# Hybrid conv and forgetting-attention layer: x loaded by quarters, summed on rows, split factor by factor

## The chip, the core and the metric

The kernel runs on one core of a Trainium2 chip. The metric is the device time of one execution, in microseconds. The core has TensorE (PE in the profile, its weight loads PEld), VectorE (DVE), ScalarE (ACT), GpSimd (POOL) and SyncE (SP), which issues most DMAs. Each takes its own queue in order and waits for others on semaphores.

## The reference

One decoder layer on 512 tokens of width 2048, cut to what matters here:

```python
def reference(x, w_in, b_in, w_dw, b_dw, g_conv_norm, b_conv_norm, w_out, b_out, g_post, b_post):
    z = jnp.einsum("bsd,de->bse", x, w_in) + b_in        # (1, 512, 2048) x (2048, 14352)
    glu_val, glu_gate, gate_c, q, k, v, f_logit, gate_a = _split_columns(z)   # 7 x 2048 and 16 columns
    y_conv = _conformer_conv(glu_val, glu_gate, w_dw, b_dw, g_conv_norm, b_conv_norm)  # 31 taps, norm, silu
    y_conv = y_conv * jax.nn.silu(gate_c)
    y_attn = _forgetting_attention(q, k, v, f_logit)     # 16 heads, causal, logits + cum[q] - cum[k],
    y_attn = y_attn * jax.nn.silu(gate_a)                #   cum = cumsum(log_sigmoid(f_logit))
    y = jnp.concatenate([y_conv, y_attn], axis=-1)
    sub = jnp.einsum("bse,ed->bsd", y, w_out) + b_out
    return _layer_norm(DN_ALPHA * x + sub, g_post, b_post)
```

## The kernel before

**Products.** Matrix products in fp32 are made of three products of rounded halves: each operand is split into a high half (rounded by ACT) and a low half (what is left, by DVE). `mm3` (L860) issues L862 to L864. `z = x w_in` goes by groups g of two column tiles of 128 (`kinds_of`, L91; 56 groups, PAIRS: q and k of a head, then v and gate_a, then val and glu; at last gate_c). A group is one 2x2 Strassen step in Winograd's form: x is cut in quarters (tokens 0 to 255 and 256 to 511, k in 0 to 1023 and 1024 to 2047), w_in's two tiles likewise in blocks B11, B12, B22, B21, and seven products m ("units", 8 k-tiles, 24 matmuls of 128x256) replace eight. ORDER (L41) gives their order, FACTOR which of x's seven factors (a11, a12, a22, ns1, s2, s3, s4) each takes, SOURCE which block. Units are numbered through: 0 to 5 in group 0, 6 is group 1's first (m = 1), 14 is group 2's m = 2 (from B21), 15 is group 1's m = 4, computed in group 2 because its source comes last. Per slot s of a group ACT rounds the weights of the unit two ahead (`high`, L582, waits until that unit's buffer is free) and DVE makes its low half (`low`, L1087).

**Sources.** sum_1 and sum_2 (DVE, L1093, L1104) and sum_3 and sum_4 (adding DMAs from POOL's queue, L506, L513) form the block sums in a ring of seven raw tiles. Group g's unit m = 4 waits for sum_4(g) (`t4_in`). In the groups with g % 3 == 1 POOL runs `masks` (L520) between sum_3 and sum_4: it waits for the bias rows of that head and adds the causal mask.

**The head of the kernel.** x is loaded whole, in five cuts of columns (`load_x`, L376, X_CUTS). For each k (0 to 7) TensorE turns eight 128x128 tiles (`turn_x`, L904), ACT copies two banks (`x_copy`, L609), DVE forms four sums (`x_sums`, L1116), ACT rounds all seven factors at once (`x_high`, L620, 128x1792) and DVE subtracts (`x_low`, L1132). TensorE takes the ten f products of that k (F_TERMS, L936 and L938) and, from k = 3 on, unit 0's products behind each. Units 1 to 5 follow behind the last k.

**Forget values.** The 16 f columns give logits in bank R5. `forget` (ACT L645, DVE L1154) makes log-sigmoid and its running sum: steps 0 and 1 (ACT) and 0 and 3 (DVE) of group 0. Then SP (L405 to L408) stores it and loads it back over the partitions as bias rows of head 0 (`load_bias`), in front of group 2's loads. `masks(0)` waits for those four loads (`bias_loaded`), DVE's row maxima of head 0 (L1249, group 2) for the masks.

The order is written out by hand in every engine's loop over g and s; a group's loads (`loads`, L325) are issued in the order B11, B12, B22, B21, each behind the use that frees its buffer.

## Time and profile before

| | us |
|---|---|
| median of 3 runs | 1664.21 (1662.56 to 1666.98) |
| profiled execution, its own time | 1665.44 |
| its span | 1663.6 |
| TensorE busy | 1603.0 (96% of the span) |
| DVE, ACT, POOL busy | 1394.4, 795.7, 234.4 |

Durations and starts are of the profiled execution, counted from the start of its span; its own time is 1.2 us above the median. A busy TensorE is not one at its peak: its matmuls overlap, so pitch (start to start) counts, not duration. The granted clock has two levels, 2.4 GHz (1.00) and 1.2 GHz (0.50); its mean over the span is 0.986.

### The profile page before, as it was taken

How to read it: one execution, taken by the hardware profiler on the slowest of the kernel's cores; microseconds unless marked ns; L12 is line 12 of the kernel's file. 1: busy time of each engine (PE TensorE's matmuls, PEld its weight loads, DVE VectorE, ACT ScalarE, POOL GpSimd, SP SyncE). 2: the span in 40 equal slices, each digit the busy share in tenths (PEclk: the TensorE clock that was granted, in tenths of full speed). 3: DMA queues.
4: the chain of work that ended last, by engine and by line, in shares of the span. 5: the costliest groups of instructions: out<-in, count | busy, mean ns of one | idle time of the engine just before them, and what ended most of it. 6: DMA issues, size and time to landing. Idle time of an engine off the chain costs nothing. (4 is left out here: it accounts for less than half of the span.)

```text
span 1663.6 us, 29190 instructions
## 1 busy us (share of the span) xinstructions
PE 1603.0 (96%) x11718; PEld 1529.3 (92%) x11718; DVE 1394.4 (84%) x1872; ACT 795.7 (48%) x1175; POOL 234.4 (14%) x231
## 2 busy tenths in 40 slices
PE   5999999999999999999999999999978899999997
PEld 4899999999999999999999999998978788888885
DVE  6669999999999999999999999999766575663358
ACT  5555454554554545545545545454544454232240
POOL 0101101101111011011111110111222002610000
PEclk9999999999999999999999999999989999999998
DMA  5666867767677676676676676766788954434232
GB/s 159 171 143 163 177 139 166 174 146 175 157 172 171 142 178 161 138 180 159 162 181 146 169 174 141 169 145 162 208 221 216 331 174 146 164 102 152 92 111 101
DMA packets 295558, 271.88 MB, mean 163 GB/s; under 512 B 11697, under 2 KB 252497, under 8 KB 294497
## 3 DMA queue, kind: packets, MB, share of 16 engines
q1 hardware_dynamic: 278288, 203.95, 42.9%
q0 software_dynamic: 17136, 66.07, 20.6%
q8 instruction: 93, 1.52, 0.4%
q14 instruction: 41, 0.34, 0.1%
HBM read 190.26 MB, written 21.00 MB: 127 GB/s over the span
## 5 line engine op out<-in xcount | busy, mean ns | idle before, releaser
L862 PE MATMUL ps<-xh,whl 128*128 128x256 f32 x3136 | 898.1, 286 | 29.1 <-ACT nu L684 16.7
L863 PE MATMUL ps<-xl,whl 128*128 128x256 f32 x3136 | 890.7, 284 | 0.0
L864 PE MATMUL ps<-xh,whl 128*128 128x256 f32 x3136 | 890.6, 284 | 0.0
L607 ACT ACTIVATE whl<-raw 128x1024 fp32r<-128x1024 f32 x392 | 415.3, 1061 | 590.5 <-PE ps L864 459.6
L1091 DVE TENSOR_TENSOR whl<-raw,whl 128x1024 fp32r<-128x1024 f32 x448 | 564.7, 1261 | 101.2 <-ACT whl L607 83.5
L862 PEld LDWEIGHTS ps<-xh,whl 128*128 128x128 f32 x3136 | 603.2, 192 | 33.2 <-ACT nu L684 17.5
L863 PEld LDWEIGHTS ps<-xl,whl 128*128 128x128 f32 x3136 | 603.4, 192 | 0.2 <-issue 0.2
L864 PEld LDWEIGHTS ps<-xh,whl 128*128 128x128 f32 x3136 | 602.9, 192 | 0.0
L1186 DVE SCALAR_TENSOR_TENSOR c_tiles<-ps,taps,c_tiles 128x511 f32<-128x511 f32 (+14 forms) x480 | 350.5, 730 | 6.9
L862 PE MATMUL ps<-whl,yh 128*128 128x512 f32 x464 | 180.6, 389 | 0.3 <-DVE yl L1363 0.3
L864 PE MATMUL ps<-whl,yl 128*128 128x512 f32 x464 | 180.5, 389 | 0.0
L863 PE MATMUL ps<-whl,yh 128*128 128x512 f32 x464 | 180.5, 389 | 0.0
L517 POOL DMA_DIRECT2D raw<-raw x56 | 48.5, 867 | 536.5 <-DVE whl L1091 466.6
L510 POOL DMA_DIRECT2D raw<-raw x56 | 48.8, 871 | 424.0 <-DVE raw L1101 414.4
L862 PEld LDWEIGHTS ps<-whl,yh 128*128 128x128 f32 x464 | 87.1, 188 | 18.5 <-issue 0.7
L864 PEld LDWEIGHTS ps<-whl,yl 128*128 128x128 f32 x464 | 87.1, 188 | 18.2
L863 PEld LDWEIGHTS ps<-whl,yh 128*128 128x128 f32 x464 | 87.1, 188 | 18.1
L1363 DVE TENSOR_TENSOR yl<-yc,yh 128x512 fp32r<-128x512 f32 x24 | 26.3, 1094 | 57.6 <-ACT yh L806 57.6
L1101 DVE TENSOR_TENSOR raw<-raw 128x1024 f32<-128x1024 f32 x56 | 71.9, 1283 | 0.6 <-DMA raw<-in_w_in_dram 0.6
L1363 DVE TENSOR_TENSOR yl<-ya,yh 128x512 fp32r<-128x512 f32 x32 | 22.1, 691 | 59.1 <-ACT yh L806 59.1
L1109 DVE TENSOR_TENSOR raw<-raw 128x1024 f32<-128x1024 f32 x56 | 68.7, 1227 | 1.9
L806 ACT ACTIVATE yh<-ya 128x512 fp32r<-128x512 f32 x32 | 20.2, 632 | 91.0 <-PE ps L864 86.3
(191 smaller groups left out, 1357.1 us busy)
## 6 DMA issues: line engine op xcount, KB each, us to landing
raw<-in_w_in_dram SPq DMA_DIRECT2D x224, 512.0 KB, 5.4
raw<-raw POOLq DMA_DIRECT2D x112, 512.0 KB, 4.9
raw<-in_w_out_dram SPq DMA_DIRECT2D x64, 512.0 KB, 3.6
probs<-forget_sums_dram SPq DMA_DIRECT2D x16, 256.0 KB, 7.2
attn_rows_dram<-tiles SPq DMA_DIRECT2D x16, 256.0 KB, 3.7
conv_rows_dram<-c_tiles SPq DMA_DIRECT2D x16, 256.0 KB, 7.2
gate_rows_dram<-tiles SPq DMA_DIRECT2D x16, 256.0 KB, 4.9
cin<-conv_rows_dram SPq DMA_DIRECT2D x16, 256.0 KB, 3.3
```

Of the source, the lines that this page charges most:

```text
L510: nc.gpsimd.dma_start(raw[:, ring(g, B12), :], raw[:, ring(g, B22), :], accum_op=ALU.add) \
L517: nc.gpsimd.dma_start(raw[:, ring(g, SUM), :], raw[:, ring(g, B21), :], accum_op=ALU.add) \
L607: nc.scalar.activation(w_high(n), source(n), ACT.Copy).then_inc(high_done, 1)
L806: nc.scalar.activation(yh[:, t % 2, :], y_tile(k), ACT.Copy).then_inc(yh_done, 1)
L862: nc.tensor.matmul(o, ah, bh, start=start, stop=False, skip_group_check=True)
L863: nc.tensor.matmul(o, ah, bl, start=False, stop=False, skip_group_check=True)
L864: return nc.tensor.matmul(o, al, bh, start=False, stop=True, skip_group_check=True)
L1091: vec.tensor_tensor(w_low(n), src, w_high(n), ALU.subtract).then_inc(low_done, 1)
L1101: vec.tensor_tensor(raw[:, ring(g, SUM), :], raw[:, ring(g, B11), :], raw[:, ring(g, B12), :], ALU.add).then_inc(t1_done, 1)
L1109: vec.tensor_tensor(o, o, raw[:, ring(g, B22), :], ALU.add).then_inc(t2_done, 1)
L1186: vec.scalar_tensor_tensor(out=o[:, n:], in0=ps[:, U_BANK, 0:SEQ - n], scalar=tap, in1=o[:, n:], op0=ALU.mult, op1=ALU.add) \
L1363: vec.tensor_tensor(yl[:, t % 2, :], y_tile(t % PER_PASS), yh[:, t % 2, :], ALU.subtract).then_inc(yl_done, 1)
```

## The change

1. x is loaded by quarters of two token tiles by 1024 columns (x11, x12, x21, x22), with the weight blocks in between; SP no longer waits for the turned and split x before dw_rows and group 1's loads.
2. The sums are formed on rows, before turning: x22 - x21 (ns1) and s2 by DVE in `x_sums`, s3 and the negative of s4 by POOL, each one operation of 128x2048. Turned are then all seven factors, in 28 banks of two k-tiles.
3. A factor's bank goes from PSUM straight to its high half (ACT, 128x512) and low half (DVE, 128x512). X_ORDER sets the order; the turns of the next factor stand between the products of units 0, 2, 3, 4 and 5, those of ns1 behind unit 1. Group 1's first unit waits for all 28.
4. f's products are regrouped so that they need factors 0, 1, 3 and 5 (with the sum of the two halves of w_f as a third weight and its negative as a fourth), each behind a unit of group 0; they end behind unit 4, in bank U_BANK. `forget` moves to group 1: ACT at s = 0 and 2, DVE at s = 1 and 3. SP's store and bias loads of head 0 move between B22 and B21 of group 2.
5. Row tiles, f_w and dw_rows lie elsewhere in memory; taps turn into R2 instead of BANK_A.

The core of the diff (declarations left out):

```diff
...
-X_CUTS = ((0, 1), (1, 2), (2, 4), (4, 6), (6, 8))
+X_ORDER = (0, 1, 3, 4, 6, 5, 2)
+X_BANKS = 4 * len(X_ORDER)
...
                     sp.wait_ge(low_done, at(g - 1, 1) + 1)
                     sp.wait_ge(t1_done, g)
                 load_block(g, B22, 1, 1)
+                if g == 2:
+                    sp.wait_ge(f_vec, 4)
+                    sp.dma_start(scratch, neg_cum[0:HEADS, :]).then_inc(cum_stored, 16)
+                    sp.wait_ge(cum_stored, 16)
+                    load_bias(0)
...
+            def load_x(q, dst, tokens, half):
+                for h in range(2):
+                    c = slice(SEQ * h, SEQ * (h + 1))
+                    src = x[0, tokens:tokens + TOK, 1024 * half + SEQ * h:1024 * half + SEQ * (h + 1)]
+                    sp.dma_start(dst[:, :, c], src.rearrange("(t p) d -> p t d", p=P)).then_inc(x_loaded[q][h], 16)
+            load_x("11", x11, 0, 0)
+            load_block(0, B11, 0, 0)
...
-            load_x(1)
+            load_x("12", x12, 0, 1)
...
+            load_block(0, B21, 1, 0)
+            load_x("21", x21, TOK, 0)
             load_block(0, B12, 0, 1)
+            load_x("22", x22, TOK, 1)
             load_block(0, B22, 1, 1)
-            load_block(0, B21, 1, 0)
             sp.dma_start(fbias[:, :], b_in[F_COL:F_COL + HEADS].rearrange("(j p) -> j p", p=1)).then_inc(fbias_loaded, 16)
-            sp.wait_ge(xt_turned, HALF)
             sp.dma_start(dw_rows[0:TAPS, :], w_dw).then_inc(dw_loaded, 16)
-            sp.wait_ge(xl_done, HALF)
             loads(1)
-            sp.wait_ge(f_vec, 4)
-            sp.dma_start(scratch, neg_cum[0:HEADS, :]).then_inc(cum_stored, 16)
-            sp.wait_ge(cum_stored, 16)
-            load_bias(0)
             for g in range(2, GROUPS):
                 loads(g)
...
+            pool.wait_ge(x_loaded["21"][0], 16)
+            pool.wait_ge(x_loaded["21"][1], 16)
+            pool.wait_ge(xt_turned, 4)
+            nc.gpsimd.tensor_tensor(x11[:, :, :], x11[:, :, :], x21[:, :, :], ALU.subtract).then_inc(s3_done, 1)
...
             for g in range(GROUPS):
                 sum_3(g)
+                if g == 0:
+                    pool.wait_ge(s2_done, 1)
+                    nc.gpsimd.tensor_tensor(x12[:, :, :], x12[:, :, :], x21[:, :, :], ALU.add).then_inc(s4_done, 1)
...
-            def x_copy(k):
-                act.wait_ge(xt_turned, k + 1)
-                if k >= 2:
-                    act.wait_ge(xl_done, k - 1)
...
-            def x_high(k):
-                act.wait_ge(x_summed, 4 * k + 4)
-                nc.scalar.activation(xh[:, :, k, :], x_tmp[k % 2][:, 1:8, :], ACT.Copy).then_inc(xh_done, 1)
-            for k in range(HALF + 1):
-                if k < HALF:
-                    x_copy(k)
-                if k >= 1:
-                    x_high(k - 1)
...
+            def x_high(f):
+                at_f = 4 * X_ORDER.index(f)
+                for b in range(4):
+                    act.wait_ge(xt_turned, X_BANKS if f == 2 else at_f + b + 1)
+                    nc.scalar.activation(xh[:, f, 2 * b:2 * b + 2, :].rearrange("p k t -> p (k t)"), ps[:, x_bank(at_f + b), :],
+                                         ACT.Copy, scale=-1.0 if f == 6 else 1.0).then_inc(xh_done, 1)
+            x_high(0)
+            high(0)
+            act.wait_ge(f_loaded, 32)
+            nc.scalar.activation(f_w[:, 0:2, :, 0:HEADS].rearrange("p a k c -> p (a k) c"),
+                                 f_raw[:, :, :, :].rearrange("p a k c -> p (a k) c"), ACT.Copy).then_inc(fw_high, 1)
+            act.wait_ge(f_summed, 1)
+            nc.scalar.activation(f_w[:, 2, :, 0:HEADS], f_sum[:, :, :], ACT.Copy).then_inc(fw_high, 1)
+            act.wait_ge(fw_low, 2)
+            act.wait_ge(vec_const, 3)
+            nc.scalar.activation(f_w[:, 3, :, :], f_w[:, 2, :, :], ACT.Copy, scale=-1.0).then_inc(fw_done, 1)
+            x_high(1)
             high(1)
...
@@ -773,15 +779,23 @@
                     n = slot_unit(g, s)
                     if n is not None:
                         high(n + 2)
-                    if g == 0 and s in (0, 1):
+                    if g == 0 and s == 0:
+                        x_high(3)
+                        x_high(4)
+                    if g == 1 and s in (0, 2):
                         forget(s)
                     evict(g, s)
+                    if g == 0 and s == 1:
+                        x_high(6)
+                    if g == 0 and s == 4:
+                        x_high(5)
                     attention(g, s)
...
+                    if g == 0 and s == 6:
                         act.wait_ge(taps_turned, 1)
...
+                if g == 1 and m == 1:
+                    pe.wait_ge(xl_done, X_BANKS)
                 for k in range(HALF):
+                    if g == 0 and m != 4 and k % 2 == 0:
+                        pe.wait_ge(xl_done, 4 * X_ORDER.index(FACTOR[m]) + k // 2 + 1)
                     last = product(n, k)
+                    if g == 0 and m in (1, 5, 6, 3, 7) and k % 2:
+                        turn_x(X_ORDER[X_ORDER.index(FACTOR[m]) + 1], k // 2)
...
+            def turn_x(f, b):
+                j = 4 * X_ORDER.index(f) + b
+                if f in quarter and b % 2 == 0:
+                    pe.wait_ge(x_loaded[quarter[f]][b // 2], 16)
+                if f in made and b == 0:
+                    pe.wait_ge(made[f], 1)
+                if j >= 4:
+                    pe.wait_ge(xl_done, j - 3)
+                for kk in range(2):
+                    for tile in range(2):
+                        o, k = TOK * kk + P * tile, 2 * b + kk
+                        last = nc.tensor.transpose(ps[:, x_bank(j), o:o + P], x_rows_of[f][:, tile, P * k:P * (k + 1)],
+                                                   ident[:, :])
                 last.then_inc(xt_turned, 1)
...
+            def f_terms(terms, first=False):
+                for w, f, r in terms:
+                    c = slice(TOK * r, TOK * (r + 1))
+                    pe.wait_ge(xl_done, 4 * X_ORDER.index(f) + 4)
+                    for k in range(HALF):
+                        nc.tensor.matmul(ps[0:F_WIDE, U_BANK, c], f_w[:, w, k, :], xh[:, f, k, :],
+                                         start=first and (w, k) == (0, 0), stop=False, skip_group_check=True)
+                        last = nc.tensor.matmul(ps[0:HEADS, U_BANK, c], f_w[:, w, k, 0:HEADS], xl[:, f, k, :],
...
+                return last
...
+            for b in range(4):
+                turn_x(0, b)
+            unit(0)
...
+            pe.wait_ge(fw_done, 1)
+            f_terms(((0, 0, 0), (2, 0, 1)), True)
...
                     if g == 0 and s == 1:
+                        for b in range(4):
+                            turn_x(3, b)
+                        f_terms(((1, 1, 0),))
+                    if g == 0 and s == 3:
+                        f_terms(((1, 3, 1),))
+                    if g == 0 and s == 5:
                         pe.wait_ge(dw_loaded, 16)
+                        pe.wait_ge(c11_done, 1)
                         for c in range(HEADS):
...
                         last.then_inc(taps_turned, 1)
+                        f_terms(((3, 5, 1),)).then_inc(f_done, 1)
...
-            def x_sums(k):
-                t = x_tmp[k % 2]
-                a21, a11, a12, a22, ns1, s2, s3, s4 = (t[:, n, :] for n in range(8))
...
-            def x_low(k):
-                dve.wait_ge(xh_done, k + 1)
-                vec.tensor_tensor(xl[:, :, k, :], x_tmp[k % 2][:, 1:8, :], xh[:, :, k, :], ALU.subtract).then_inc(xl_done, 1)
...
+            def x_low(f):
+                at_f = 4 * X_ORDER.index(f)
+                if f == 2:
+                    dve.wait_ge(taps_turned, 1)
+                for b in range(4):
+                    dve.wait_ge(xh_done, at_f + b + 1)
+                    hi = xh[:, f, 2 * b:2 * b + 2, :].rearrange("p k t -> p (k t)")
+                    lo = xl[:, f, 2 * b:2 * b + 2, :].rearrange("p k t -> p (k t)")
+                    if f == 6:
+                        vec.scalar_tensor_tensor(out=lo, in0=ps[:, x_bank(at_f + b), :], scalar=-1.0, in1=hi,
+                                                 op0=ALU.mult, op1=ALU.subtract).then_inc(xl_done, 1)
+                    else:
+                        vec.tensor_tensor(lo, ps[:, x_bank(at_f + b), :], hi, ALU.subtract).then_inc(xl_done, 1)
...
+            x_low(0)
+            low(0)
+            dve.wait_ge(f_loaded, 32)
+            vec.tensor_tensor(f_sum[:, :, :], f_raw[:, 0, :, :], f_raw[:, 1, :, :], ALU.add).then_inc(f_summed, 1)
+            dve.wait_ge(fw_high, 2)
...
+            x_low(1)
+            low(1)
             sum_1(0)
...
+            def x_sums():
+                for h in range(2):
+                    dve.wait_ge(x_loaded["21"][h], 16)
+                    dve.wait_ge(x_loaded["22"][h], 16)
+                vec.tensor_tensor(xs1[:, :, :], x22[:, :, :], x21[:, :, :], ALU.subtract).then_inc(ns1_done, 1)
+                dve.wait_ge(ns1_done, 1)
+                dve.wait_ge(s3_done, 1)
+                vec.scalar_tensor_tensor(out=x21[:, :, :], in0=x11[:, :, :], scalar=-1.0, in1=x22[:, :, :],
+                                         op0=ALU.mult, op1=ALU.subtract).then_inc(s2_done, 1)
...
@@ -1340,13 +1367,24 @@
                     conv(i, before)
                     if n is not None:
                         low(n + 2)
+                        if n == 0:
+                            x_sums()
+                            x_low(3)
                         if n + 2 < UNITS and UNIT_OF[n + 2][1] == 5:
                             sum_2(UNIT_OF[n + 2][0])
+                        if n == 0:
+                            x_low(4)
+                        if n == 1:
+                            x_low(6)
                     if s == 5 and g < GROUPS - 1:
                         sum_1(g + 1)
-                    if g == 0 and s in (0, 3):
+                    if g == 1 and s in (1, 3):
                         forget(s)
                     evict(g, s)
+                    if g == 0 and s == 4:
+                        x_low(5)
+                    if g == 0 and s == 6:
+                        x_low(2)
...
```

**SP, from group 1's B11 on.** `raw<-in_w_in_dram` are w_in's blocks, `forget_sums_dram` the running sums. Before:

```order
L321 DMA raw<-in_w_in_dram 128x8x128
L321 DMA raw<-in_w_in_dram 128x8x128 [waits t1_done,low_done]
L321 DMA raw<-in_w_in_dram 128x8x128 [waits t3_in0,low_done]
L406 DMA forget_sums_dram<-neg_cum 16x512 [waits f_vec]
L352 DMA probs<-forget_sums_dram 128x128 [waits cum_stored]
L352 DMA probs<-forget_sums_dram 128x256
L352 DMA probs<-forget_sums_dram 128x384
L352 DMA probs<-forget_sums_dram 128x512
L321 DMA raw<-in_w_in_dram 128x8x128 [waits low_done]
L321 DMA raw<-in_w_in_dram 128x8x128 [waits t4_in0]
```

In the changed kernel (from group 2's B11; group 1's four stand ahead of it):

```order
L332 DMA raw<-in_w_in_dram 128x8x128 [waits t3_in0,low_done]
L332 DMA raw<-in_w_in_dram 128x8x128 [waits low_done]
L332 DMA raw<-in_w_in_dram 128x8x128 [waits t4_in0]
L332 DMA raw<-in_w_in_dram 128x8x128 [waits t1_done,low_done]
L350 DMA forget_sums_dram<-neg_cum 16x512 [waits f_vec]
L368 DMA probs<-forget_sums_dram 128x128 [waits cum_stored]
L368 DMA probs<-forget_sums_dram 128x256
L368 DMA probs<-forget_sums_dram 128x384
L368 DMA probs<-forget_sums_dram 128x512
L332 DMA raw<-in_w_in_dram 128x8x128 [waits t3_in1,low_done]
L332 DMA raw<-in_w_in_dram 128x8x128 [waits low_done]
```

Behind group 1's loads stood the store and the bias loads; now B11, B12 and B22 of group 2 go first, and B21 waits behind them.

**POOL's queue at the start.** L510 (now L518) is sum_3, L517 (now L525) sum_4, `probs<-probs,mask` the masks of head 0. Before:

```order
L510 DMA raw<-raw 128x1024 [waits b22_in0,t1_done,const_done]
L517 DMA raw<-raw 128x1024 [waits b21_in0,low_done]
L510 DMA raw<-raw 128x1024 [waits b22_in1,t1_done]
L525 TENSOR_TENSOR probs<-probs,mask 128x128 [waits bias_loaded]
L525 TENSOR_TENSOR probs<-probs,mask 128x128 x3
L517 DMA raw<-raw 128x1024 [waits b21_in1,low_done]
L510 DMA raw<-raw 128x1024 [waits b22_in0,t1_done]
```

In the changed kernel:

```order
L555 TENSOR_TENSOR x<-x 128x2048 [waits x21_loaded1,xt_turned,x21_loaded0,const_done]
L518 DMA raw<-raw 128x1024 [waits b22_in0,t1_done]
L561 TENSOR_TENSOR x<-x 128x2048 [waits s2_done]
L525 DMA raw<-raw 128x1024 [waits b21_in0,low_done]
L518 DMA raw<-raw 128x1024 [waits b22_in1,t1_done]
L533 TENSOR_TENSOR probs<-probs,mask 128x128 [waits bias_loaded]
L533 TENSOR_TENSOR probs<-probs,mask 128x128 x3
L525 DMA raw<-raw 128x1024 [waits b21_in1,low_done]
```

Two sums of x came in, one ahead of sum_3(0) and one behind it; masks(0) and sum_4(1) stand as they did.

**DVE around the forget values.** L1091 (now L1117) is `low`, L1109 (now L1133) sum_2. Before, in group 0, from sum_2(0) on:

```order
L1109 TENSOR_TENSOR raw<-raw 128x1024 [waits b22_in0,low_done]
L1159 SCALAR_TENSOR_TENSOR f_tmp<-ps,fbias,f_low 16x512 [waits fbias_loaded,f_act]
L1091 TENSOR_TENSOR whl<-raw,whl 128x1024 [waits high_done] x2
L1163 SCALAR_TENSOR_TENSOR c_tiles<-f_tmp 16x512 [waits f_act]
L1167 SCALAR_TENSOR_TENSOR c_tiles<-csum,c_tiles 16x512 [waits f_vec,vec_const]
L1169 TENSOR_SCALAR neg_cum<-c_tiles 16x512 [waits f_vec]
L1170 MEMSET csum 128x512
L1211 TENSOR_TENSOR tiles<-ps,p 128x256 [waits unit_done,p1_done]
```

In the changed kernel, in group 1, behind its sum_2 (L1263 is k's low half, L1238 the eviction c11):

```order
L1186 SCALAR_TENSOR_TENSOR f_tmp<-ps,fbias,f_low 16x512 [waits fbias_loaded,f_act]
L1117 TENSOR_TENSOR whl<-raw,whl 128x1024 [waits high_done]
L1263 TENSOR_TENSOR parts<-tiles,parts 128x512 [waits kh_done]
L1117 TENSOR_TENSOR whl<-raw,whl 128x1024 [waits high_done]
L1190 SCALAR_TENSOR_TENSOR c_tiles<-f_tmp 16x512 [waits f_act]
L1194 SCALAR_TENSOR_TENSOR c_tiles<-csum,c_tiles 16x512 [waits f_vec,vec_const]
L1196 TENSOR_SCALAR neg_cum<-c_tiles 16x512 [waits f_vec]
L1197 MEMSET csum 128x512
L1238 TENSOR_TENSOR tiles<-ps,p 128x256 [waits unit_done,p1_done]
L1117 TENSOR_TENSOR whl<-raw,whl 128x1024 [waits high_done] x2
```

The three operations on 16 partitions moved from behind low(4) to behind low(11).

## Rows read from the trace of the kernel before

**Rows 1.** What TensorE waited for up to 68 us: total, times, longest

```profile
PE ps L936 <- DVE xl L1134: 10.8, 6, 2.6
PE ps L913 <- DMA x_rows<-in_x_dram: 9.1, 3, 4.7
```

**Rows 2.** Windows: busy per engine (x instructions), PEclk, DMA share, GB/s

```profile
2.00:25.00 23.00, 12.90 (x65) 10.55 (x66) 13.01 (x22) 11.21 (x19) 0.00 (x0) 1.00 1.01 281
4.63:67.20 62.57, 45.66 (x306) 40.35 (x307) 44.73 (x59) 35.80 (x46) 2.46 (x3) 0.92 0.56 152
...
95.03:1120.00 1024.97, 1024.97 (x8448) 1020.95 (x8447) 981.53 (x1382) 536.90 (x833) 144.23 (x169) 1.00 0.69 161
```

**Rows 3.** Timeline of TensorE: start, us, engine, line, op, tiles [idle before]

```profile
4.66 1.09 PE L913 MATMUL ps<-ident,x_rows 128*128 128x128 f32 x4 [4.66 <-DMA x_rows<-in_x_dram]
...
24.66 0.32 PE L936 MATMUL ps<-xh,f_w 128*48 128x256 f32 x1 [2.60 <-DVE xl L1134]
...
25.87 0.60 PE L913 MATMUL ps<-ident,x_rows 128*128 128x128 f32 x4
26.30 0.60 PE L916 MATMUL ps<-ident,x_rows 128*128 128x128 f32 x4
...
67.20 0.28 PE L862 MATMUL ps<-xh,whl 128*128 128x256 f32 x1
...
89.27 0.28 PE L862 MATMUL ps<-xh,whl 128*128 128x256 f32 x1
...
95.03 0.29 PE L862 MATMUL ps<-xh,whl 128*128 128x256 f32 x1
```

**Rows 4.** Groups by shape, ACT and DVE: count, busy us, mean ns

```profile
L607 ACT ACTIVATE whl<-raw 128x1024 fp32r<-128x1024 f32 x392 | 415.3, 1061 | 590.5 <-PE ps L864 459.6 <-DVE raw L1109 73.7 <-DMA raw<-in_w_in_dram 46.9
L720 ACT ACTIVATE vh<-ps 128x512 fp32r<-128x512 f32 x16 | 9.3, 582 | 0.0
...
L1109 DVE TENSOR_TENSOR raw<-raw 128x1024 f32<-128x1024 f32 x56 | 68.7, 1227 | 1.9
L1265 DVE TENSOR_TENSOR vl<-ps,vh 128x512 fp32r<-128x512 f32 x16 | 11.0, 685 | 0.0
L1134 DVE TENSOR_TENSOR xl<-w_even,xh 128x1792 fp32r<-128x1792 f32 x4 | 8.1, 2026 | 0.0
```

**Rows 5.** Timeline of POOL and DVE where both run on SBUF

```profile
1441.10 4.60 POOL L573 TENSOR_TENSOR res<-res,bout_b 128x2048 f32<-128x2048 f32 x1
...
1441.26 5.53 DVE L1091 TENSOR_TENSOR whl<-raw,whl 128x1024 fp32r<-128x1024 f32 x1 [0.26 <-ACT whl L588]
```

**Rows 6.** Windows around 1210 us, columns as in Rows 2

```profile
1204.40:1210.00 5.60, 0.00 (x1) 0.01 (x1) 0.52 (x2) 1.48 (x3) 0.00 (x0) 0.75 1.01 265
1210.00:1214.00 4.00, 4.00 (x18) 4.00 (x19) 3.66 (x3) 0.46 (x1) 1.44 (x1) 0.50 1.09 285
```

**Rows 7.** Timeline of the forget chain: ACT, DVE, SP and POOL

```profile
53.80 0.62 ACT L652 ACTIVATE f_tmp<-f_tmp 16x512 f32<-16x512 f32 x1
...
56.39 0.72 ACT L656 ACTIVATE f_tmp<-f_tmp,one 16x512 f32<-16x512 f32 x1
...
59.73 0.67 DVE L1163 SCALAR_TENSOR_TENSOR c_tiles<-f_tmp 16x512 f32<-16x512 f32 x1
...
62.20 0.33 SPq L406 DMA_DIRECT2D forget_sums_dram<-neg_cum  x1
63.80 1.77 SPq L352 DMA_DIRECT2D probs<-forget_sums_dram  x4
...
72.37 2.85 POOL L525 TENSOR_TENSOR probs<-probs,mask 128x128 f32<-128x128 f32 x4 [4.83 <-DMA probs<-forget_sums_dram]
76.71 0.87 POOL L517 DMA_DIRECT2D raw<-raw  x1 [1.49 <-DVE whl L1091]
```

**Rows 8.** L517, POOL's sum_4, by source line

```profile
DMA to landing us min/median/max: 4.5/4.9/7.4
```

**Rows 9.** The page's DMA issues: count, KB each, us to landing

```profile
raw<-in_w_in_dram SPq DMA_DIRECT2D x224, 512.0 KB, 5.4
```

170 lines of the change are left out of this document (49 added, 121 removed).

## The prediction

> **What bounds the kernel now.** I read the waits of TensorE first. Up to 68 us it waits 10.8 us for DVE's low halves of x and 9.1 us for x itself [rows 1]. The windows come next. While the loads run (2 to 25 us) the DMA engines move 281 GB/s; between 4.63 and 67.20 TensorE is busy for 45.66 of 62.57 us; from 95.03 to 1120 it is busy all the time, and DVE for 981.53 of 1024.97 us [rows 2]. So what is gained or lost before 95 us moves the end by as much: a dense TensorE can't catch up. Last, TensorE's timeline [rows 3]: the first transposes start at 4.66, group 1's first unit (unit 6 from 0; I call its start U) at 67.20, unit 13 behind the first head's scores at 89.27, unit 15 at 95.03. A unit takes (95.03 - 89.27)/2 = 2.88 us at the higher of the clock's two levels, and unit 15 starts at U + 27.83. Any change has to be judged by two numbers: where U goes, and whether unit 15 still starts at U + 27.8.
>
> **The head, part by part.** What goes: eight steps, one for each k, in which a bank pair is turned, copied (ACT), summed (DVE), rounded (ACT) and subtracted (DVE, 2.03 us [rows 4]); TensorE only does f products and two turns in a step (24.66 to 26.9, then it waits [rows 3]). What comes: 28 banks (7 factors, 4 banks each), 112 transposes instead of 64, in banks of 0.43 us (26.30 - 25.87 [rows 3]), so 12.0 us; the 80 f products stay, at 0.12 us each (ten between 24.66 and 25.87 [rows 3]); six units, 17.3 us. A bank costs ACT 0.58 us and DVE 0.68 us [rows 4], of which some 0.1 overlaps the next. The sums on rows are two DVE operations of 128x2048, 2.3 us each by the 1792 elements in 2.03 us [rows 4], and two on POOL, 4.6 us each [rows 5].
>
> Landings: x's first 0.52 MB before are there at 4.66; after that I count bytes at 281 GB/s [rows 2, 3]. In the new order: x11 6.5, block B11 8.4, x12 12.6, B21 14.8, x21 18.5, B12 20.3, x22 24.1, B22 25.9.
>
> The queues, followed in this order, give:
> - Unit 0 starts when B11's low half is made: ACT ends xh of factor 0 near 9.1, rounds B11 to 10.1 and DVE subtracts to 11.3 (1.06 and 1.23 us [rows 4]). TensorE is at the lower clock there. I let it rise near 16.5. Unit 0 with four banks ends at 18.3, the f products of factor 0 at 22.5.
> - POOL's first sum runs from 18.5 (x21) to 23.1. DVE's low half of B21 wants to start at 20.1. What two such operations do to each other stands in [rows 5]: a DVE operation on two SBUF inputs, started 0.16 us behind a POOL sum of 4.60 us, took 5.53 us instead of 1.2. So it ends at 24.3: unit 1 runs 24.4 to 27.3.
> - sum_1 25.5, high and low of unit 2 to 27.8, x22 - x21 to 30.1, the next sum to 32.4. TensorE waits 2.8 us for factor 3. DVE: low halves of factor 3 to 34.9; then sum_2, which POOL's second sum (32.4 to 37.0) holds to 38.2; factor 4 to 40.7; low(3) to 41.9. Unit 2 and its banks end at 38.3, f at 40.2, wait 1.8.
> - Unit 3 with factor 6's banks 42.0 to 46.6. ACT takes high(4) only behind all four banks, so low(4) ends at 49.7 and the eviction before unit 4 at 49.9: wait 3.3. Unit 4 to 54.5, taps and f to 57.8, unit 5 to 62.4. Unit 6 waits for all 28 banks: four of ACT and four of DVE behind the last turn, to 65.7: wait 3.3.
>
> So U = 65.7 with the clock high from 16.5 on. In a gap of 5.60 us the clock fell, and the 4 us behind it, at the lower level (0.50), held 18 matmuls, where 0.12 us each makes 33 [rows 6]: nearly 2 us lost. Four gaps of 1.8 to 3.3 us follow here; I add 2.5 us, with 0 and 8 as ends. **U = 68.2, against 67.2: +1.0.** Lowest: no hold by POOL (-3.2 and -1.2 us) and no fall of the clock, U near 61; highest 74.
>
> On the hold the Trainium skill (SBUF — State Buffer, section "SBUF: two separate sides") says that the shared port pair is an exclusive lock, taken by a DVE operation only with two SBUF inputs or in a 2-port mode. By that the low halves read from PSUM go free, as I have them; no row here shows that pair. Were they held as well, factor 3's would end at 39.5 instead of 34.9, and U would be some 4 us later: inside my upper end.
>
> **The forget chain.** It is the part of the change that looks free. It moves from group 0 (steps 0 and 3) into group 1 (ACT at 0 and 2, DVE at 1 and 3), and its end, the four bias loads, moves behind B22 of group 2. Before, the last forget operation ended and the store was issued at 62.20, U - 5.0; the masks began on POOL at 72.37, U + 5.2, and sum_4(1) was issued at 76.71, U + 9.5 [rows 7]. POOL's queue is unchanged: masks(0), then sum_4(1), the source of unit 15 (its t4_in). Now, from U on:
> - high(9) waits for unit 6: U + 3.1 to 4.2; low(9) 5.5, sum_2(1) 6.6, the bias sum of f 7.3.
> - ACT's Abs, Exp, table load and Ln take 57.11 - 53.80 = 3.3 us [rows 7], behind high(10) at 7.7: to U + 11.0. high(11) to 12.1, low(11) to 13.3.
> - DVE's three forget operations end where the store is issued, 62.20 - 59.73 = 2.47 us [rows 7]: U + 15.75. Low(12) stands behind them and ends at 17.9; unit 12 loses 0.6 us.
> - Store to masks 10.2 us, masks 2.85 [rows 7]: U + 28.8. Issue to landing of such a sum 4.9 us [rows 8]: U + 33.7. High, low and c22, which unit 15 waits for too, 2.75 us (1.06, 1.23 and some 0.4 for c22 and the hand-overs): U + 36.45.
>
> Unit 15 was due at U + 27.8, so **8.6 us**. Part of it shows one unit earlier: B21 of group 2 stands in SP's queue behind the bias loads, so it is issued no sooner than 65.57 - 62.20 = 3.4 us behind the forget end [rows 7], at U + 19.1; with the 5.4 us of such a load [rows 9] and the bias loads ahead of it I take U + 27.5, where unit 14, due at U + 25.5, needs it 2.3 us earlier: it waits some 4 us. Behind unit 15 ACT and DVE have lost their lead of two units: the row maxima, Exp and high(17) follow one another there; I add 1.1 us (0 to 2.5), my estimate of what stands between. The two gaps, 4 and 3 us, cost clock as in [rows 6]: 1.5 (0 to 3.5). **Together +11.2.** Ends: landing 4.5 to 7.4 [rows 8], masks without contention 1 us less, bias loads 2 us quicker on an emptier queue, no clock loss: +6; the other way +16.
>
> Nothing hides it: DVE's position behind low(11) alone (unit 9's start + 2.6 + 2.45 = U + 13.7) leaves 5 us of stall with every other term at its lower end. B21 of group 2 lost its cover for the same reason.
>
> **The rest** costs nothing: POOL had 1.5 us idle before sum_4 and has no other early work; dw_rows, fbias and the cols come long before use; memory is only laid out anew.
>
> **Sum.** The profiled execution took 1665.4 us (span 1663.6), 1.2 above the median. 1665.4 + 1.0 + 11.2 = 1677.6; less 1.2, **1676 us**, about 0.7% slower.
>
> **Rivals.**
> - Both terms at their low side (0.17): U near 62 to 64, stall +7: the head's gain pays for the stall, 1660 to 1668. For it: 16.9 us of waits in the head really exist. Against: seven factors one behind the other, each with an ACT and a DVE pass before the next unit.
> - The head gets dense (0.08). If TensorE never waited behind the start of unit 0, the rest of the head would take only its own work: 10.3 us of turns, 9.6 of f, 2 small, 17.3 of units and 3 of low clock, 42 us from 11.3: U = 53. Then -14 + 10 = -4, 1660, and with the stall at 5, 1655. It decides for faster from U below about 56. Against it: the waits found above are bare chains, ACT behind a bank and DVE behind ACT, with no other work that could give way.
> - Worse than forecast (0.13): the PSUM readers are held too and every gap costs clock, 1683 to 1692. Here also belongs a sentence of the Trainium skill (TensorE: Matmul & The Clock Gate, "Part 4: PE-mode transpose"), by which transposes don't lift the clock. Row 24.66 to 26.30 speaks against it (f products and turns alone, at 0.12 us a matmul); were it so, the head's 40 us of work would double and the result pass 1690.
> - The change doesn't do what it says (0.02): the forget values are wanted later than I think, no stall; then only U's shift counts, 1665.
>
> **How the numbers follow.** Forecast 0.60. The range 1662 to 1684 leaves out the dense head and the worst case, about 0.2. A measurement of this kernel can tell 0.3% from no change, 5 us. Faster by more: 0.08. Within: 0.20 (the first and last rival, and the forecast's edge). Slower: 0.72.
>
> **What would show it.** The store of the forget sums some 16 us behind unit 6's start, masks near U + 26, and TensorE idle before units 14 and 15 by 7 to 9 us together, released by a low half behind DMA. In the head: unit 6 between 65 and 70, DVE operations of 3 to 6 us beside POOL's two sums, waits before units 3, 4 and 6. I am wrong if unit 15 starts by U + 30, or if U is below 60.

## The result

The changed kernel took 1676.97 us (median; 1673.43 to 1678.42), the kernel before, on the same chip, 1665.17 (1662.56 to 1668.28). The ratio is 1.0067, with a 95% interval of 1.0049 to 1.0086: 11 us slower, 8 to 14. The prediction said 1676, slower. The profiled execution has a span of 1674.8 us, against 1663.6. All medians here are of executions in the chip's fast state; one slow execution of the kernel called "masks last" below (2605.86 us) is left out.

What TensorE waited for up to 115 us in the changed kernel (total, times, longest), where the kernel before had 10.8 us for low halves of x, 9.1 us for x (both [rows 1]) and 1.6 us for low halves of weights. In all it is 25.4 us for 21.5, only 3.9 more, so waiting alone doesn't make up 11 us. The five longest:

```profile
PE ps L876 <- DVE whl L1117: 9.9, 4, 4.7
PE ps L938 <- DMA x<-in_x_dram: 4.8, 1, 4.8
PE ps L876 <- DVE xl L1153: 3.4, 1, 3.4
PE ps L876 <- ACT p L683: 2.9, 1, 2.9
PE ps L938 <- DVE xs L1175: 2.7, 1, 2.7
```

L938 is a turn, L876 the first matmul of a product; `xl` is a low half of x, `whl` a low half of weights, `xs` the row sum ns1, `p` an eviction by ACT. The first row holds four waits, the longest of 4.7 us. It stands in group 2. TensorE's timeline, its starts in the head and in group 2, against [rows 3]:

```profile
24.57 0.38 PE L876 MATMUL ps<-xh,whl 128*128 128x256 f32 x1 [1.86 <-DVE whl L1117]
...
30.39 3.57 PE L938 MATMUL ps<-ident,xs 128*128 128x128 f32 x16 [2.69 <-DVE xs L1175]
...
43.35 0.36 PE L876 MATMUL ps<-xh,whl 128*128 128x256 f32 x1 [1.06 <-ACT p L671]
...
51.13 0.58 PE L876 MATMUL ps<-xh,whl 128*128 128x256 f32 x1 [2.94 <-ACT p L683]
...
68.82 0.55 PE L876 MATMUL ps<-xh,whl 128*128 128x256 f32 x1 [3.37 <-DVE xl L1153]
...
101.51 0.36 PE L876 MATMUL ps<-xh,whl 128*128 128x256 f32 x1 [4.70 <-DVE whl L1117]
...
106.39 0.38 PE L876 MATMUL ps<-xh,whl 128*128 128x256 f32 x1 [0.28 <-DVE tiles L1254]
```

These are unit 1, the turns of factor 3, units 3, 4 and 6, then 14 and 15. Unit 6, U of the prediction, starts at 68.82 (before 67.20, +1.62). Unit 15 starts at 106.39, U + 37.57, where it was U + 27.83: so 9.74 us are lost between the two: 4.70 in one wait before unit 14, only 0.28 before unit 15 (for c22, behind low(15)), and the other 4.8 because TensorE ran slower. Of these, 3.0 stand between U and that wait (unit 6 alone took 5.25 us for 2.88), 1.7 in unit 14. The windows, against [rows 2]:

```profile
2.00:25.00 23.00, 15.43 (x93) 14.21 (x94) 12.40 (x15) 8.18 (x17) 4.60 (x1) 1.00 1.03 300
66.00:70.00 4.00, 1.18 (x5) 1.22 (x6) 3.81 (x6) 3.08 (x6) 0.00 (x0) 0.73 0.01 3
68.82:74.00 5.18, 5.18 (x24) 5.18 (x25) 1.31 (x2) 0.28 (x1) 0.00 (x0) 0.50 0.62 167
70.00:90.00 20.00, 19.99 (x150) 19.81 (x149) 11.63 (x15) 10.82 (x15) 0.00 (x0) 0.88 0.32 83
100.00:105.00 5.00, 3.49 (x18) 3.52 (x19) 1.77 (x3) 1.41 (x3) 0.83 (x1) 0.70 0.97 184
115.00:1130.00 1015.00, 1014.94 (x8363) 1010.68 (x8362) 974.49 (x1373) 529.00 (x817) 144.29 (x167) 1.00 0.69 162
```

Columns as in rows 2. The loads ran at 300 GB/s instead of 281. The clock column is the new thing: 0.73 around unit 6's wait, 0.50 over unit 6 itself (the row of 5.18 us), 0.88 over 70 to 90 us, 0.70 around unit 14's wait. From 115 us on TensorE is dense again.

A landmark for the middle of the kernel is POOL's sum_4 of group 20 (the rows of before, then of after):

```profile
493.58 0.86 POOL L517 DMA_DIRECT2D raw<-raw  x1 [11.66 <-DMA raw<-in_w_in_dram]
```

```profile
506.25 0.86 POOL L525 DMA_DIRECT2D raw<-raw  x1 [11.64 <-DVE whl L1117]
```

It stands 12.67 us later, and so do those of groups 10, 40 and 49, to 0.02 us: nothing is gained or lost in the dense part. I call this the **dense shift** and use it below, because it is free of what the last 450 us do. Behind 1176 us, where both kernels wait for loads again, 1.5 us are given back in these two executions (span +11.2). Other kernels below give back more, or lose some: a dense shift and a time can differ by some 3 us.

### The profile page after: what moved, and what is told of

It is laid out like the page before. It is cut to its first block and busy times, and to the rows that moved or that the text cites. A ratio compares the mean times of both kernels' runs of the same rounds, so it can differ in the third digit from the quotient of the medians.

```text
span 1674.8 us, 29286 instructions
## 1 busy us (share of the span) xinstructions
PE 1612.9 (96%) x11766; PEld 1540.7 (92%) x11766; DVE 1397.8 (83%) x1863; ACT 790.2 (47%) x1180; POOL 242.7 (14%) x233
## 5 line engine op out<-in xcount | busy, mean ns | idle before, releaser
L876 PE MATMUL ps<-xh,whl 128*128 128x256 f32 x3136 | 903.5, 288 | 42.4 <-ACT nu L690 13.9
L623 ACT ACTIVATE whl<-raw 128x1024 fp32r<-128x1024 f32 x392 | 415.0, 1060 | 591.8 <-PE ps L878 448.4
L1117 DVE TENSOR_TENSOR whl<-raw,whl 128x1024 fp32r<-128x1024 f32 x448 | 565.7, 1263 | 108.7 <-ACT whl L623 88.6
L876 PEld LDWEIGHTS ps<-xh,whl 128*128 128x128 f32 x3136 | 606.6, 193 | 48.1 <-ACT nu L690 14.7
L876 PE MATMUL ps<-whl,yh 128*128 128x512 f32 x464 | 180.6, 389 | 0.3 <-DVE yl L1401 0.3
L525 POOL DMA_DIRECT2D raw<-raw x56 | 48.5, 866 | 533.9 <-DVE whl L1117 475.7
L876 PEld LDWEIGHTS ps<-whl,yh 128*128 128x128 f32 x464 | 87.1, 188 | 18.7 <-issue 0.7
L518 POOL DMA_DIRECT2D raw<-raw x56 | 49.1, 876 | 379.3 <-DVE raw L1125 369.6
L1401 DVE TENSOR_TENSOR yl<-yc,yh 128x512 fp32r<-128x512 f32 x24 | 30.7, 1281 | 53.4 <-ACT yh L820 53.4
L1133 DVE TENSOR_TENSOR raw<-raw 128x1024 f32<-128x1024 f32 x56 | 70.6, 1260 | 1.9
L604 ACT ACTIVATE whl<-raw 128x1024 fp32r<-128x1024 f32 x56 | 58.5, 1046 | 13.2 <-DMA raw<-in_w_out_dram 13.2
```

The source lines that it names most:

```text
L518: nc.gpsimd.dma_start(raw[:, ring(g, B12), :], raw[:, ring(g, B22), :], accum_op=ALU.add) \
L525: nc.gpsimd.dma_start(raw[:, ring(g, SUM), :], raw[:, ring(g, B21), :], accum_op=ALU.add) \
L604: nc.scalar.activation(w_high(n), raw_out(t), ACT.Copy).then_inc(high_done, 1)
L623: nc.scalar.activation(w_high(n), source(n), ACT.Copy).then_inc(high_done, 1)
L876: nc.tensor.matmul(o, ah, bh, start=start, stop=False, skip_group_check=True)
L1117: vec.tensor_tensor(w_low(n), src, w_high(n), ALU.subtract).then_inc(low_done, 1)
```

## The forget chain in the trace

From ACT's Ln to unit 15's weights in the changed kernel: ACT's Ln, the first of DVE's last three operations, SP's store and B21 of group 2 (with the four loads behind it), POOL's masks and sum_4(1), ACT's high(14), and high(15) with high(16). It answers to [rows 7]:

```profile
81.54 0.72 ACT L662 ACTIVATE f_tmp<-f_tmp,one 16x512 f32<-16x512 f32 x1
...
84.39 0.67 DVE L1190 SCALAR_TENSOR_TENSOR c_tiles<-f_tmp 16x512 f32<-16x512 f32 x1
...
86.85 0.33 SPq L350 DMA_DIRECT2D forget_sums_dram<-neg_cum  x1
...
90.31 24.52 SPq L332 DMA_DIRECT2D raw<-in_w_in_dram  x5
...
97.47 1.68 POOL L533 TENSOR_TENSOR probs<-probs,mask 128x128 f32<-128x128 f32 x4 [34.94 <-DMA probs<-forget_sums_dram]
99.11 0.84 POOL L525 DMA_DIRECT2D raw<-raw  x1
...
99.05 1.06 ACT L623 ACTIVATE whl<-raw 128x1024 fp32r<-128x1024 f32 x1 [11.51 <-DMA raw<-in_w_in_dram]
103.69 2.00 ACT L623 ACTIVATE whl<-raw 128x1024 fp32r<-128x1024 f32 x2 [3.59 <-DMA raw<-raw]
```

Set against the prediction, from U = 68.82: store U + 18.0 (said 15.75), masks U + 28.65 (25.95), end of the masks U + 30.3 (28.75), sum_4(1) landed and high(15) started U + 34.9 (33.7), unit 15 U + 37.57 (36.45). The chain is the one that was described. The store is 2.3 us late because unit 6 ran at the lower clock (0.50 from 68.82 to 74.00), and high(9), low(9) and all behind them wait for unit 6's end. The masks took 1.68 us instead of 2.85, which gives 1.2 back.

B21 of group 2 was issued at 90.31 and high(14) could read it at 99.05, U + 30.2 (said 27.5). So unit 14 waited 4.70 us, and then ran at the lower clock (0.70 from 100 to 105); by the time that it ended sum_4(1) had landed. The wait that I had put in front of both units in equal parts stood nearly whole in front of unit 14. Which of the two chains is the longer can't be told from that trace, since each hides the other. That is what the first experiments are for.

## Experiments on the forget chain

**Only the late chain.** The kernel before, its head untouched, with the end of the forget chain moved as in the change:

```diff
@@ SP, in loads(g), behind B22; taken out behind loads(1)
+                if g == 2:
+                    sp.wait_ge(f_vec, 4)
+                    sp.dma_start(scratch, neg_cum[0:HEADS, :]).then_inc(cum_stored, 16)
+                    sp.wait_ge(cum_stored, 16)
+                    load_bias(0)
@@ ACT
-                    if g == 0 and s in (0, 1):
+                    if (g, s) in ((0, 0), (1, 2)):
                         forget(s)
@@ DVE
-                    if g == 0 and s in (0, 3):
+                    if (g, s) in ((0, 0), (1, 3)):
                         forget(s)
```

> The kernel before with only the end of the forget chain moved as the change moves it: ACT's Abs, Exp and Ln to group 1's slot 2, DVE's three operations to slot 3, store and bias loads of head 0 between B22 and B21 of group 2. x's loading and the head stay. Theory (the late forget chain stalls group 2 by itself): unit 6 stays at 67 us, the store stands at 83, masks(0) at 93, unit 14 and unit 15 wait for 7 to 9 us together; 8 to 11 us above the kernel before, 1673 to 1676. Rival (the loss comes from the new head, the forget chain has cover): within 3 us of the kernel before.

It took 1671.04 us beside 1665.49 of before (ratio 1.0040, 1.0028 to 1.0052); dense shift 7.92. Unit 6, store, masks and unit 14:

```profile
66.00 0.28 PE L863 MATMUL ps<-xh,whl 128*128 128x256 f32 x1
...
81.62 0.33 SPq L339 DMA_DIRECT2D forget_sums_dram<-neg_cum  x1
...
92.77 1.69 POOL L526 TENSOR_TENSOR probs<-probs,mask 128x128 f32<-128x128 f32 x4 [27.67 <-DMA probs<-forget_sums_dram]
...
96.61 0.55 PE L863 MATMUL ps<-xh,whl 128*128 128x256 f32 x1 [5.04 <-DVE whl L1092]
```

The late chain alone makes the kernel slower, and by the same two waits (5.04 before unit 14, 0.67 before unit 15). Together they are 5.7 us; I expected 7 to 9. The stall is 7.9 us in the dense part, or 9.1 counted from unit 6, which started 1.2 us earlier (66.00) than in the kernel before; I expected 8 to 11 over the whole time, and 5.6 were measured. Unit 6 ran at the higher clock here, and the store stood 15.62 us behind it, as the prediction has it (15.75). 3.7 us of the 7.9 are given back behind 1200 us in the profiled execution (its last sum_4 is only 4.25 later than that of before), where the kernel waits for loads and not for TensorE.

**The chain early.** The changed kernel, with the forget steps where ACT and DVE idle:

```diff
@@ ACT
-                    if g == 1 and s in (0, 2):
-                        forget(s)
+                    if g == 1 and s == 0:
+                        forget(2)
@@ ACT, g == 0 and s == 6, behind taps
+                        forget(0)
                         x_high(2)
@@ DVE
-                    if g == 1 and s in (1, 3):
-                        forget(s)
                     evict(g, s)
+                    if g == 1 and s == 0:
+                        forget(3)
@@ DVE, g == 0 and s == 6
+                        forget(1)
                         x_low(2)
```

> The changed kernel with the forget chain started as soon as its logits are there: ACT's copy and DVE's first operation ahead of factor 2's halves in group 0, the rest in slot 0 of group 1, where both engines idle for 5 us. Queues of SP and POOL as in the changed kernel. Theory: the store stands near 74, masks near 84.5, no unit waits before unit 17; of the shift of 12.7 us only the head's 1.6 and the low clock behind unit 6 (2.6) stay: 1667 to 1671. Rival (the bias loads in front of B21, or the masks in front of sum_4, cost wherever the chain ends): above 1674.

1669.74 us (ratio 1.0021, 1.0011 to 1.0031), dense shift 3.79. Store, masks and the only wait of TensorE between 69 and 120 us:

```profile
74.05 0.33 SPq L350 DMA_DIRECT2D forget_sums_dram<-neg_cum  x1
...
86.50 3.74 POOL L533 TENSOR_TENSOR probs<-probs,mask 128x128 f32<-128x128 f32 x4 [24.09 <-DMA probs<-forget_sums_dram]
...
104.22 0.35 PE L877 MATMUL ps<-xh,whl 128*128 128x256 f32 x1 [0.21 <-DVE whl L1118]
```

With the queues of SP and POOL as the change has them, 8.9 us of the 12.67 are gone. The order on those queues costs next to nothing as long as the forget values come in time. What stays, 3.8 us, is unit 6's start (68.70, +1.5), the low clock in unit 6 (4.44 us for 2.88, +1.6) and 0.7 us behind unit 15, whose cause I didn't follow up.

**B21 first; masks last; both.** On the changed kernel, with the late chain left as it is:

```diff
@@ SP (first and third kernel): the four lines of store and load_bias(0) behind, not ahead of
                 load_block(g, B21, 1, 0)
@@ POOL (second and third kernel)
-                if g < HEAD_GROUPS and g % 3 == 1:
+                if g < HEAD_GROUPS and g % 3 == 1 and g > 1:
                     masks(g // 3)
                 sum_4(g)
+                if g == 1:
+                    masks(0)
```

> The changed kernel with B21 of group 2 issued before the store and the bias loads. Theory (two chains hang on the forget values): unit 14 waits 1 us at most, unit 15 then waits some 5 for sum_4(1) and starts near 106 as before; time within 2 us of the changed kernel, 1675 to 1678. Rival (B21's place in SP's queue is the whole stall, as unit 14's wait of 4.7 us in the trace suggests): 5 to 7 us faster, 1670 to 1672.

1677.43 us (1.0071, 1.0056 to 1.0086), no faster than the change, as expected. The wait has moved to unit 15:

```profile
103.57 0.58 PE L876 MATMUL ps<-xh,whl 128*128 128x256 f32 x1 [5.56 <-DVE tiles L1254]
```

> The changed kernel with masks(0) behind sum_4(1) on POOL and nothing else. Theory (two chains side by side, of which unit 14's through B21 is as long): sum_4(1) lands before unit 15 is due, but unit 14 still waits 4 to 5 us for B21 and its low half; only the later waits shrink: dense part 0.5 to 2.5 us earlier than in the changed kernel for the same start of unit 6, time 1674 to 1677. Rival (POOL's order is the whole stall): 1668 to 1671, as with both edits.

1674.57 us (1.0057, 1.0038 to 1.0076), the median of three. The wait before unit 14 is as long as it was:

```profile
99.73 0.36 PE L878 MATMUL ps<-xh,whl 128*128 128x256 f32 x1 [4.60 <-DVE whl L1119]
```

> The changed kernel with B21 of group 2 ahead of the store and with masks(0) behind sum_4(1) on POOL. Theory: both chains to units 14 and 15 are cut; a third stays, the row maxima of head 0 on DVE wait for the masks until 99 instead of 92 and hold the low half of unit 16 and 17: a stall of 1 to 4 us, 1668 to 1673. Rival (the row maxima have no lead to lose either): as slow as the changed kernel, 1675 or more.

1669.85 us (1.0028, 1.0019 to 1.0038); the profiled execution, 1667.21, is its fastest. The only wait of TensorE in group 2:

```profile
101.85 0.35 PE L878 MATMUL ps<-xh,whl 128*128 128x256 f32 x1 [0.16 <-DVE whl L1119]
```

The head of these kernels is the same, but their unit 6 starts at different times (below), so the dense shift is read from U: (dense shift) - (U - 67.20).

| kernel | U | dense shift | from U | span |
|---|---|---|---|---|
| changed kernel | 68.82 | 12.67 | 11.05 | +11.2 |
| late chain alone | 66.00 | 7.92 | 9.12 | +4.7 |
| B21 first | 67.14 | 10.16 | 10.22 | +12.2 |
| masks last | 67.15 | 9.10 | 9.15 | +9.2 |
| both | 66.00 | 1.43 | 2.63 | +1.8 |
| chain early | 68.70 | 3.79 | 2.29 | +4.9 |

(The late chain alone has the head of the kernel before. The span is that of the profiled execution, less 1663.6.)

From U, one edit alone brings 0.8 or 1.9 us, both together 8.4. (The spans tell less: B21 first loses 2.0 us behind the dense part, where the changed kernel gains 1.5.) So there are two chains side by side behind the forget values, bias loads to B21 to unit 14 and bias loads to masks to sum_4(1) to unit 15, about 1 us apart in length (10.22 and 9.15 from U); either keeps the stall when the other is cut. The third, the row maxima that wait for the masks, has cover: with both edits no cost can be told from the early chain's (2.63 beside 2.29 from U, one execution each; I had allowed 1 to 4), though the masks ran from 93.26 to 95. I had expected them up to 99; unit 6 was early in this execution, so the edit was tried less hard than planned. Two kernels set the forget chain's own price from U: 11.05 - 2.29 = 8.8 us in the changed kernel, 9.1 alone.

## Experiments on the head

A DVE operation that is kept from running by one on POOL I call held. What DVE and POOL do beside each other in the changed kernel, against [rows 5]:

```profile
18.83 4.60 POOL L555 TENSOR_TENSOR x<-x 128x2048 f32<-128x2048 f32 x1 [16.96 <-PE ps L938]
...
20.26 4.25 DVE L1117 TENSOR_TENSOR whl<-raw,whl 128x1024 fp32r<-128x1024 f32 x1 [0.26 <-ACT whl L623]
...
32.75 4.59 POOL L561 TENSOR_TENSOR x<-x 128x2048 f32<-128x2048 f32 x1 [5.72 <-DVE x L1178]
...
32.58 2.74 DVE L1153 TENSOR_TENSOR xl<-ps,xh 128x512 fp32r<-128x512 f32 x4
35.23 3.19 DVE L1133 TENSOR_TENSOR raw<-raw 128x1024 f32<-128x1024 f32 x1
```

Low(1) started at 20.26 with POOL's s3 running until 23.43, and ended at 24.51, 1.08 behind POOL's end. Sum_2 started at 35.23, POOL's s4 ended at 37.34, sum_2 at 38.42, again 1.08 behind. In [rows 5] it is 1446.79 - 1445.70 = 1.09. Wherever it starts, the operation of 128x1024 ends the same 1.08 or 1.09 us behind POOL's end, a little less than the 1.22 it takes alone. So it doesn't run slower beside POOL, it waits and then runs. The four low halves of x between them read PSUM and took 2.74 us beside POOL's sum; in a kernel below they took 2.47 wholly beside one (34.61, without s3 in the loads' time) and in the last kernel 2.47 without one (34.24): not held. This is the pair that no row of before showed. It agrees with the Trainium skill (SBUF — State Buffer, "SBUF: two separate sides"), by which a VectorE operation takes the shared lock only with two SBUF inputs or in a 2-port mode.

**Without s3.**

```diff
-            nc.gpsimd.tensor_tensor(x11[:, :, :], x11[:, :, :], x21[:, :, :], ALU.subtract).then_inc(s3_done, 1)
+            nc.gpsimd.tensor_tensor(x11[:, 0, 0:P], x11[:, 0, 0:P], x21[:, 0, 0:P], ALU.subtract).then_inc(s3_done, 1)
```

> The changed kernel with POOL's first sum (s3) cut from 128x2048 to 128x128 elements, so part of factor 5 is left out; nothing else changed. Theory (the SBUF sum on POOL holds DVE's operation on two SBUF inputs): low(1) takes 1.2 us instead of 4.25, unit 1 starts at 22.7 instead of 24.57, factor 3's turns at 27.6 instead of 30.39, unit 6 two to three us earlier than with the same clock. Rival (the 4.25 us come from the loads' traffic): low(1) stays above 3 us and factor 3's turns start near 30.

Low(1) and the turns of factor 3:

```profile
20.98 1.23 DVE L1117 TENSOR_TENSOR whl<-raw,whl 128x1024 fp32r<-128x1024 f32 x1 [0.26 <-ACT whl L623]
...
28.08 1.97 PE L938 MATMUL ps<-ident,xs 128*128 128x128 f32 x16 [1.78 <-DVE xs L1175]
```

Low(1) takes 1.23 us, the turns start 2.3 us earlier (28.08 for 30.39), unit 6 at 65.43. That is 3.4 earlier than in the changed kernel, but 1.7 earlier than in "B21 first" and "masks last" (67.14, 67.15), whose turns of factor 3 also took 1.97 us: the hold is worth some 2 us here, the rest is clock. The traffic of the loads was the same (341 GB/s from 18 to 25 us, 340 with s3), so the hold, not the loads, made the 4.25 us. The one profiled execution took 1674.1 us.

**High(4) and low(4) early.** On the kernel with the early chain:

```diff
@@ ACT (DVE likewise, with low(4) and x_low(6)); skipped in slot 3
                     if g == 0 and s == 1:
+                        high(4)
                         x_high(6)
```

> The changed kernel with the forget chain early (as in e2_forget_early) and with high(4) and low(4) ahead of factor 6's halves on ACT and DVE, where both engines idle. Theory: the 2.9 us of wait in front of unit 4 fall to 1 or less, unit 6 starts near 66.5, time 1667 to 1669. Rival (the chain turn, high, low of factor 6 sets unit 4's start by itself): same as e2_forget_early within 1 us, 1669 to 1671.

1668.41 us (1.0018, 1.0009 to 1.0028), dense shift 2.97, beside 3.79 with the early chain alone. In time the two can't be told apart. Unit 4 still waits 2.00 us, where I expected 1 or less, and unit 6 starts at 67.88, not 66.5:

```profile
50.02 0.39 PE L879 MATMUL ps<-xh,whl 128*128 128x256 f32 x1 [2.00 <-ACT p L683]
```

It waited for low(4) no more, but for the eviction of p5, which ACT takes behind factor 6's four halves and high(5). The edit freed one of two things in the row.

**s3 out of the loads' time.** Also on the early chain:

```diff
@@ DVE, x_sums: s2 from ns1, with low(2) ahead of it
-                dve.wait_ge(s3_done, 1)
-                vec.scalar_tensor_tensor(out=x21[:, :, :], in0=x11[:, :, :], scalar=-1.0, in1=x22[:, :, :],
+                low(2)
+                vec.scalar_tensor_tensor(out=x21[:, :, :], in0=xs1[:, :, :], scalar=-1.0, in1=x11[:, :, :],
@@ POOL, behind s4; factor 5 is then turned with its sign changed, as factor 6 is
+                    nc.gpsimd.tensor_tensor(x11[:, :, :], x21[:, :, :], x22[:, :, :], ALU.add).then_inc(s3_done, 1)
```

> The changed kernel with the forget chain early and with POOL's s3 taken out of the loads' time: s2 is formed by DVE from ns1 and x11, and POOL forms the negative of s3 (s2 + x22) behind s4; low(2) stands behind ns1. Theory: low(1) is not held, factor 3's turns start near 26.5, unit 2 near 31 instead of 35.6; POOL's two sums then lie side by side at 30 to 39 and hold sum_2 and low(3), which gives 1 to 2 us back. Unit 6 at 63 to 65, time 1663 to 1666. Rival (the landing of x22 sets factor 3, not the hold): turns of factor 3 at 28 or later, time 1668 or more.

1668.78 us (1.0024, 1.0013 to 1.0036); unit 6 at 66.78, outside the 63 to 65 and the 1663 to 1666 that I expected. Half of the theory held: the turns of factor 3 started at 25.52 and unit 2 at 29.67, five to six us earlier. The gain went here:

```profile
29.02 4.58 POOL L556 TENSOR_TENSOR x<-x 128x2048 f32<-128x2048 f32 x1 [1.28 <-DVE x L1178]
33.57 5.53 POOL L558 TENSOR_TENSOR x<-x 128x2048 f32<-128x2048 f32 x1
...
31.24 3.44 DVE L1133 TENSOR_TENSOR raw<-raw 128x1024 f32<-128x1024 f32 x1
34.61 2.47 DVE L1153 TENSOR_TENSOR xl<-ps,xh 128x512 fp32r<-128x512 f32 x4
37.00 3.18 DVE L1117 TENSOR_TENSOR whl<-raw,whl 128x1024 fp32r<-128x1024 f32 x1
...
40.28 0.55 PE L876 MATMUL ps<-xh,whl 128*128 128x256 f32 x1 [3.95 <-issue]
```

Sum_2 is held to POOL's first end (33.60 + 1.08 = 34.68), low(3) to its second (39.10 + 1.08 = 40.18), and unit 3 waits 3.95 us for it. I had allowed 1 to 2. The second sum took 5.53 us instead of 4.58, and sum_2 ran in its first 1.1 us: this looks like POOL waiting for DVE in the same way. Two sums back to back cost DVE two holds, and POOL one.

**Both, and unit 6 behind one bank.** The two edits together, and

```diff
@@ PE, unit(n); factor 2's banks are turned in the order R1_ODD, BANK_A, BANK_B, BANK_C
                 if g == 1 and m == 1:
-                    pe.wait_ge(xl_done, X_BANKS)
+                    pe.wait_ge(xl_done, X_BANKS - 3)
+                if g == 0 and m == 4:
+                    pe.wait_ge(xl_done, X_BANKS)
```

> e7_no_s3_first and e9_high4 together, and unit 6 waits for the one bank of factor 2 that shares its PSUM bank, not for all four (the first product of factor 2, unit 8, waits for the rest). Theory: unit 6 at 58 to 62 and no wait in group 2, time 1656 to 1661, below the kernel before. Rival (the head stays a chain of seven factors, one ACT and one DVE pass each, whatever stands beside it): unit 6 above 64, 1663 or more.

1665.18 us (0.9996, 0.9986 to 1.0007): level with the kernel before. Units 3, 4 and 6:

```profile
40.58 0.35 PE L880 MATMUL ps<-xh,whl 128*128 128x256 f32 x1 [3.97 <-issue]
...
48.97 0.39 PE L880 MATMUL ps<-xh,whl 128*128 128x256 f32 x1 [1.99 <-ACT p L684]
...
63.49 0.36 PE L880 MATMUL ps<-xh,whl 128*128 128x256 f32 x1 [1.57 <-DVE xl L1159]
```

Unit 6's wait fell from 3.37 to 1.57, as meant; the gap before unit 3 (3.97) and the eviction before unit 4 (1.99) stayed. Unit 6 at 63.49 is outside the 58 to 62 that I expected, and the time above the 1656 to 1661. Both gaps had names by now, so one more kernel takes them away.

**No hold, p5 early.**

```diff
@@ POOL, behind sum_3(0); s4 is taken out here
+                    pool.wait_ge(low_done, 5)
+                    pool.wait_ge(x_loaded["22"][1], 16)
+                    nc.gpsimd.tensor_tensor(x11[:, :, :], s2_rows[:, :, :], x22[:, :, :], ALU.add).then_inc(s3_done, 1)
@@ DVE, behind sum_2(0); s2_rows, which s2 now goes to, lies where factor 5's low half comes later
+                            dve.wait_ge(s2_done, 1)
+                            vec.tensor_tensor(x12[:, :, :], x12[:, :, :], s2_rows[:, :, :], ALU.add).then_inc(s4_done, 1)
                             x_low(4)
@@ ACT, g == 0 and s == 1 (skipped in slot 4)
+                        evict(0, 4)
                         high(4)
                         x_high(6)
```

> e8_head with no POOL sum beside a DVE operation on two SBUF inputs: s2 goes to memory of its own (where factor 5's low half comes later), DVE forms the negative of s4 behind sum_2, POOL forms the negative of s3 behind low(4), while DVE only reads PSUM; and ACT evicts p5 right behind p1, ahead of factor 6's halves. Theory (the 4 us gap of e8_head in front of unit 3 is the hold of sum_2 and low(3), the 2 us in front of unit 4 is the eviction behind high(5)): unit 3 starts near 38.7, unit 4 without a wait of more than 0.5, unit 6 at 59 to 61, time 1659 to 1662. Rival (with the hold gone the turn, high, low chain of factors 4 and 6 is as late): unit 6 above 62.5, 1664 or more.

1658.45 us beside 1666.15 of before (ratio 0.9960, 0.9946 to 0.9975), dense shift -7.60. DVE from sum_2 on, units 3 and 6:

```profile
30.91 1.21 DVE L1141 TENSOR_TENSOR raw<-raw 128x1024 f32<-128x1024 f32 x1
32.04 2.28 DVE L1386 TENSOR_TENSOR x<-x,s_rows 128x2048 f32<-128x2048 f32 x1
34.24 2.47 DVE L1161 TENSOR_TENSOR xl<-ps,xh 128x512 fp32r<-128x512 f32 x4
...
37.95 0.36 PE L882 MATMUL ps<-xh,whl 128*128 128x256 f32 x1 [1.94 <-issue]
...
57.52 0.36 PE L882 MATMUL ps<-xh,whl 128*128 128x256 f32 x1 [1.57 <-DVE xl L1161]
```

Sum_2 takes 1.21 us, s4 on DVE 2.28; unit 3 starts at 37.95 behind 1.94 us of waiting, unit 4 without a wait, unit 6 at 57.52; both are earlier than the 38.7 and the 59 to 61 that I expected, and the time is below the 1659 to 1662. The two gaps are read apart by their rows: unit 3 came 2.6 us earlier than in e8_head (40.58), and the 1.99 us in front of unit 4 are gone. This kernel loads and sums x as the change does, and is by the medians 18.5 us faster than the changed kernel and 7.7 faster than the one before. From U it still loses 2.1 us (-7.60 for a unit 6 that is 9.68 earlier), at a clock of 1.00 from 68 to 95 us; I didn't follow that up.

## Why the prediction was right, and where its terms were off

- **Direction and size.** 1676 was forecast, 1677.0 measured; +12.2 by its sum and 12.67 in the dense part. Two terms, U and the stall, were to make it up, and they did. The stretch behind 1176 us was put at nothing and gave 1.5 us back; that the number came within 1 us has some luck in it, here and in the stall below.
- **U: +1.0 said, +1.62 measured.** The queues' ledger held to some tenths for 30 us: unit 0 at 11.3 (11.37), low(1) to 24.3 (24.5), unit 1 24.4 (24.57), factor 3's turns 30.1 (30.39). The clock rose where the text let it: unit 0's matmuls followed one another every 0.21 us up to 16.4 us, every 0.12 behind. (The clock column reads 1.00 over all of 2 to 25 us, so it doesn't show this stretch.) Units 3 and 4 came at 43.35 and 51.13 for 42.0 and 49.9, though their waits were 1.06 and 2.94 for 1.8 and 3.3. The 2.5 us set aside for clock come out as 3.1 if all that the sum leaves open (68.82 - 65.7) is put down to it.
- **The clock at U is no constant.** Kernels with this head started unit 6 at 66.00, 67.14, 67.15, 68.70 and 68.82. Two places make the difference. From factor 3's turns to unit 2 it took 5.26 us in the two late ones, whose turns came behind a wait of 2.7 us, and 3.7 in the three others, behind one of 1.2. And from unit 4 to unit 5 it took 8.2 us in the first, 9.4 to 9.7 in the others. The ends 61 to 74 held them all.
- **The stall: 8.6 said from U to unit 15, 9.74 measured.** Behind it came 1.31 (12.67 - 11.36), where the sum added 1.1 for the lost lead and 1.5 for clock. So +11.2 met 11.05 because one term was 1.1 too small and the other two together 1.3 too large; that they cancel is luck. The mis-sized step is the one from U to the store, 2.3 us too short: it counted unit 6 at the higher clock, right behind a wait for which the same text charged low clock. The late chain alone bears this out: its unit 6 ran at the higher clock, and its store came at U + 15.62 for 15.75. Shorter masks took half of the 2.3 back. The clock of the two gaps was charged on top, where it doesn't belong: unit 14 did take 106.39 - 101.51 - 0.28 = 4.6 us instead of 2.88, but sum_4(1) was still on its way, so unit 15 lost nothing more by it.
- **A share that isn't the forget chain's.** The sum gave all of the 11.2 to it. With the chain early, 2.3 us from U are still lost, 1.6 of them in unit 6's low clock. The text charged the clock of all four gaps of the head to U, but what the gap before unit 6 costs falls behind U; in the changed kernel it is also what made the store late.
- **Where the stall stands.** "It waits some 4 us" for unit 14 was 4.70. That unit 15 would wait as long again was wrong, for B21 landed 2.7 us later than the text had it. The sign "TensorE idle before units 14 and 15 by 7 to 9 us together" failed with it: 4.98 were measured, and slower running filled the rest. The two chains are nearly the same length, so the sum came near with either as the last.
- **The cover.** "Nothing hides it" is borne out by the two kernels that have the late chain with one link cut, and by the late chain alone, which costs 9.1 us from U on the old head.
- **The rivals.** The low side of both terms would need U at 62 to 64; no run with this head has it. The dense head was given 0.08, "bare chains, with no other work that could give way". For this order of work that is so, but as a statement on the head it is too strong: e10_best reaches U = 57.5 with the same loads, the same 28 banks and the same f products. The waits were chains of order (a sum beside another, an eviction behind four halves, a wait for four banks where one counts), of which I had seen the first and taken it as given. The third rival's doubled head, with transposes that don't lift the clock, did not come: from 33 to 43 us, turns, products and f products mixed, the granted clock was 0.96. No run here has turns alone for more than some 4 us, so what they do by themselves is not shown.

## What to carry to other kernels

A step moved behind "its first use is far away" must be followed to every queue that stands behind it: here a store of 16 rows held two units by two different queues, and cutting either alone brought next to nothing. Place large GpSimd operations on SBUF where VectorE only reads PSUM; each one beside a VectorE operation with two SBUF inputs costs VectorE the rest of its duration. When a wait is removed, read the same row for what else the instruction waits for before pricing the gain.

## What was not expected of the hardware

- The hold seems to work in both directions: the second of two 128x2048 sums on POOL took 5.53 and 5.55 us instead of 4.60, both times where a DVE operation of 1.2 us came in between the two. It was seen, not tried by itself.
- A VectorE operation of 128x1024 on two SBUF inputs (1.22 us alone) that meets a running GpSimd sum ends 1.08 or 1.09 us behind it, in five cases, wherever it had started: it waits for the whole sum and then runs.
- With the same instructions, the 10 us from 43 to 53 us of the head ran at a granted clock of 0.83, 0.89 or 1.00 in different executions, and unit 6 started up to 2.8 us apart. A difference of some us between two heads says nothing until the waits, and not only the starts, are compared.
- 7.9 us lost at 95 us were only 5.6 in the time of the late-chain kernel. The stretch behind 1176 us, where the kernel waits for loads, gave 3.2 back there (span +4.7) and 1.5 in the changed kernel, but took 2.0 more in "B21 first": it doesn't do so reliably.
